# Delta and differential attention in one stage of 49 slots, with a level's pairs formed and copied ahead of the first half turn

## What the reference computes

```python
h = rms_norm_2(x, pre_mix_w[l]); u = h @ w_in[l]
y_conv  = conv_module(...)
y_diff  = diff_attention(dq, dk, dv, lambdas..., l)     # 6 heads, 12 maps of width 32
y_delta = gated_deltanet(gqkv, gz, b_f, b_b, a_f, a_b, ...)   # 6 heads, two directions
x = x + rms_norm_2(concat(y_conv, y_diff, y_delta) @ w_out[l], ...)
x = x + rms_norm_2(square(relu(rms_norm_2(x) @ w_ff1)) @ w_ff2, ...)
```

```python
p = softmax(s - slopes[:, None, None] * dist); a = p[:, :, 0] - lam * p[:, :, 1]
o = einsum("bhqk,bkhe->bqhe", a, vf)
```

## Time and profile before

| what | value |
|---|---|
| median of 3 runs | 4210.27 us (4207.33 to 4212.7) |
| span of the profiled execution | 4209.9 us |
| PE busy | 3901.8 us (93%) |
| PEld busy | 3126.2 us (74%) |
| DVE busy | 2270.4 us (54%) |
| ACT busy | 1414.5 us (34%) |
| POOL busy | 237.8 us (6%) |
| mean granted TensorE clock | 0.943 |

### The profile page before, as it was taken

How to read it: one execution, slowest core, us unless ns; L and a number is a source line. 1 busy time by engine, 2 the same in 40 slices (tenths; PEclk the granted TensorE clock), 3 DMA queues, 4 the chain that set the end, 5 groups by cost and what they waited for, 6 DMA issues and landing times. The chain is left out here.

```text
span 4209.9 us, 49789 instructions
## 1 busy us (share of the span) xinstructions
PE 3901.8 (93%) x20649; PEld 3126.2 (74%) x20649; DVE 2270.4 (54%) x3424; ACT 1414.5 (34%) x2074; POOL 237.8 (6%) x212
## 2 busy tenths in 40 slices
PE   7998799999999999899999989889998989898998
PEld 4884667888888777578877778557786768666876
DVE  5625755554564333362267666753475856664375
ACT  2115633111443121252254222432364322343264
POOL 0000210000000000000000032000000023000000
PEclk9998889999999999999999999789999989799998
DMA  5500013343112111123232100022232200012231
GB/s 203 171 31 10 6 41 100 128 134 117 57 56 83 58 58 58 40 81 100 82 100 84 53 4 1 6 71 90 90 100 68 69 7 1 6 61 70 90 100 60
DMA packets 254721, 288.90 MB, mean 69 GB/s; under 512 B 6757, under 2 KB 226940, under 8 KB 254518
## 3 DMA queue, kind: packets, MB, share of 16 engines
q1 hardware_dynamic: 252437, 281.84, 20.8%
q10 hardware_dynamic: 2080, 4.19, 0.3%
HBM read 283.92 MB, written 2.10 MB: 68 GB/s over the span
## 5 line engine op out<-in xcount | busy, mean ns | idle before, releaser
L458 PE MATMUL banks<-h_halves,w_halves 128*128 128x512 f32 x3824 | 1437.4, 376 | 83.1 <-DVE h_halves L257 42.2
L459 PE MATMUL banks<-h_halves,w_halves 128*128 128x512 f32 x3824 | 1429.7, 374 | 0.0
L460 PE MATMUL banks<-h_halves,w_halves 128*128 128x512 f32 x3824 | 1422.9, 372 | 0.0
L458 PEld LDWEIGHTS banks<-h_halves,w_halves 128*128 128x128 f32 x3824 | 735.1, 192 | 234.7 <-issue 84.9
L460 PEld LDWEIGHTS banks<-h_halves,w_halves 128*128 128x128 f32 x3824 | 732.4, 192 | 127.8
L459 PEld LDWEIGHTS banks<-h_halves,w_halves 128*128 128x128 f32 x3824 | 734.6, 192 | 121.1 <-issue 0.5
L257 DVE TENSOR_TENSOR w_halves<-work,w_halves 128x2048 fp32r<-128x2048 f32 (+1 forms) x215 | 488.2, 2271 | 468.7 <-ACT w_halves L252 468.4
L252 ACT ACTIVATE w_halves<-work 128x2048 fp32r<-128x2048 f32 (+1 forms) x215 | 407.2, 1894 | 535.7 <-PE banks L460 401.9
L252 ACT ACTIVATE h_halves<-kept 128x512 fp32r<-128x512 f32 (+1 forms) x520 | 332.5, 666 | 313.4 <-PE banks L460 234.8
L257 DVE TENSOR_TENSOR h_halves<-kept,h_halves 128x512 fp32r<-128x512 f32 (+1 forms) x520 | 361.2, 736 | 138.6 <-ACT h_halves L252 137.9
L950 DVE SCALAR_TENSOR_TENSOR kept<-kept 128x512 f32<-128x512 f32 x280 | 188.2, 744 | 7.7 <-DMA kept<-in_mod_w 7.7
(11 more groups left out here) (367 smaller groups left out, 4548.4 us busy)
## 6 DMA issues: line engine op xcount, KB each, us to landing
work<-in_w_ff SPq DMA_DIRECT2D x64, 1024.0 KB, 5.4
work<-in_ffn_w_in SPq DMA_DIRECT2D x44, 1024.0 KB, 5.1
kept<-in_mod_w SPq DMA_DIRECT2D x40, 1024.0 KB, 5.2
work<-in_odd_w_in SPq DMA_DIRECT2D x24, 1024.0 KB, 5.1
work<-in_w_in SPq DMA_DIRECT2D x24, 1024.0 KB, 5.2
work<-in_ffn_w_out SPq DMA_DIRECT2D x16, 1024.0 KB, 5.2
work<-in_even_w_in SPq DMA_DIRECT2D x13, 1024.0 KB, 5.3
work<-in_odd_w_out SPq DMA_DIRECT2D x8, 1024.0 KB, 5.2
```

The lines of the kernel that those rows point to most:

```text
L458: nc.tensor.matmul(o, low[:, k - a, fc], rh[:, tc], start=(k == 0), stop=False)
L459: nc.tensor.matmul(o, high[:, k - a, fc], rl[:, tc], start=False, stop=False)
L460: mm = nc.tensor.matmul(o, high[:, k - a, fc], rh[:, tc], start=False, stop=(k == K - 1))
```

## The change

`diff_stage` is gone and `delta_stage` becomes `mixer_stage`, which carries the 24 attention steps in the 49 slots: a step starts every second slot. With `step_at(t, lag)`, slot t does the scores of step (t + 2) / 2 at its end, the maximum and the exponentials one slot later, the scaling and the subtraction two later, the turns three later, the weighing four later. Every step's turn is made in two parts of two transposes through half a bank, each copied by ScalarE.

PSUM banks are dealt anew: pairs and products share one whole bank (they had two halves of two banks), the turned blocks have one bank (before: two), preparation and outputs one each, the small state products one in all (before: two, alternating), attention three. So a level is no longer cut in halves, except for the turn, whose second half waits until ScalarE has emptied the bank.

The level's mask is applied on GpSimd ahead of time to the Gram matrix (`masked_level`), and VectorE's masking of the pairs is replaced by a copy of the pairs on ScalarE (`pairs_copy`). The first level's pairs are a transpose. In a slot TensorE issues pairs, half turn 0, half turn 1; ScalarE copies pairs, half 0, half 1. The scaling of the second map and the copying out of results go from VectorE to ScalarE. The dummy matmuls are gone. A set has 50 semaphores. The split operands and the buffers of attention get new places in SBUF.

```diff
+PAIR0 = U0 + 26 * SEQ
+    level_bank, x_bank, prep_bank, out_bank = (core.ps[:, b, :] for b in range(4))
+    score_bank = lambda m: core.ps[:, 5 + m, :]
+    turn_bank = core.ps[:, 7, 0:2 * P]
...
+            def pairs(h, lv):
+
+                m = level_of(h, lv)
+                pe.wait_ge(level_masked, m + 1)
+                if m:
+                    pe.wait_ge(u_done, m)
+                for c in range(4):
+                    o, s = level_bank[:, cc(c)], pl.level[m % 3][:, cc(c)]
+                    if lv:
+                        mm = nc.tensor.matmul(packed(o, lv), s, chunk_blocks(h, lv, c), start=True, stop=True)
+                    else:
+                        mm = nc.tensor.transpose(o, s, core.ident())
                 mm.then_inc(pt_done, 1)
...
             def turn(h, lv, e):
 
+                pe.wait_ge(u_done, level_of(h, lv))
+                if turn_of(h, lv, e):
+                    pe.wait_ge(x_done, turn_of(h, lv, e))
...
+            prepare(0, 0)
+            pe.wait_ge(v_copied, 1)
+            pe.wait_ge(dist_made, 1)
+            scores(0)
+            for step in range(1, 4):
                 prepare(0, step)
-                for _ in range((1, 1, 2, 0)[step]):
-                    nc.tensor.matmul(core.ps[:, 7, :], core.sb(ONES0, P), core.x(0)[:, LAT], start=True, stop=True)
             for h in range(H + 1):
                 for lv in range(LV):
+                    t = level_of(h, lv)
                     if h < H:
-                        for e in range(2):
-                            pairs(h, lv, e)
+                        pairs(h, lv)
                     if h < H and lv:
-                        for e in range(2):
-                            turn(h, lv, e)
+                        turn(h, lv, 0)
+                    if h < H and lv:
+                        turn(h, lv, 1)
                     before(h, lv)
+                    attend(t, 0)
                     if h < H and lv:
-                        for e in range(2):
-                            products(h, lv, e)
+                        products(h, lv)
                     behind(h, lv)
+                    attend(t, 1)
...
+            for t in range(slots):
+                h, lv = divmod(t, LV)
+                if step_at(t, 4) is not None:
+                    copy(step_at(t, 4), 1)
+                if h < H and lv:
+                    pairs_copy(h, lv)
+                    kept(h, lv, 0)
+                    kept(h, lv, 1)
+                if step_at(t, 2) is not None:
+                    rescale(step_at(t, 2))
+                if step_at(t, 3) is not None:
+                    copy(step_at(t, 3), 0)
+                if step_at(t, 4) is not None:
+                    out(step_at(t, 4))
+                if step_at(t, 1) is not None:
+                    s = step_at(t, 1)
+                    exps(s)
+                    if s in split_at:
+                        split(split_at[s])
...
+            def masked_level(h, lv):
+
+                m = level_of(h, lv)
+                if lv == 0:
+                    pool.wait_ge(s_ready, h + 1)
+                if m >= 3:
+                    pool.wait_ge(pt_done, m - 2)
+                nc.gpsimd.tensor_tensor(c4(pl.level[m % 3]), c4(pl.s[h % 2]), mat(pl.pairs[:, cc(lv)]),
+                                        ALU.mult).then_inc(level_masked, 1)
...
+            def update(h, lv):
+                u = blocks(h, lv)
...
+                nc.vector.tensor_tensor(u, u, packed(level_bank, lv), ALU.subtract).then_inc(u_done, 1)
...
+                if step_at(t, 1) is not None:
+                    top(step_at(t, 1))
+                if step_at(t, 2) is not None:
+                    invert(step_at(t, 2))
...
+                if h < H:
+                    update(h, lv)
+                if step_at(t, 2) is not None:
+                    subtract(step_at(t, 2))
...
-    delta_stage(core, nc, pl)
-    diff_stage(core, nc, a, l)
+    mixer_stage(core, nc, a, l, pl)
```

More of the change, by code:

```diff
@@ L33 @@
 NEG = -1.0e30
-SET = 49
+SET = 50
 GW = 256
@@ L2773, in __init__ @@
         self.u, self.s = [take(1024) for _ in range(3)], [take(512), take(512)]
+        self.level = [take(512) for _ in range(3)]
         self.x, self.pt, self.bm = take(512), take(512), [take(512), take(512)]
@@ new lines, in turn_step, with weigh @@
+            def turn_step(s, part):
+                if part == 0:
+                    pe.wait_ge(subtracted, s + 1)
+                    if s:
+                        pe.wait_ge(out_done, s)
+                else:
+                    pe.wait_ge(turned_copied, 2 * s + 1)
+                for j in range(2):
+                    mm = nc.tensor.transpose(turn_bank[:, cc(j)], pl.both[s % 2][:, cc(2 * part + j)], core.ident())
+                mm.then_inc(turned, 1)
+            def weigh(s):
+                h, i = steps[s]
+                pe.wait_ge(turned_copied, 2 * s + 2)
+                for j in range(4):
+                    mm = nc.tensor.matmul(weigh_bank(half(h)), pl.vt_diff[:, j * DIFF_W + h * HD:j * DIFF_W + (h + 1) * HD],
+                                          pl.at[s % 2][:, cc(j)], start=(j == 0), stop=(j == 3))
+                mm.then_inc(weighted, 1)
@@ new lines, in attend @@
+            def attend(t, place):
+                if place == 0:
+                    for s, work in ((step_at(t, 3), lambda s: turn_step(s, 0)), (step_at(t, 4), weigh)):
+                        if s is not None:
+                            work(s)
+                else:
+                    for s, work in ((step_at(t, 0), scores), (step_at(t, 3), lambda s: turn_step(s, 1))):
+                        if s is not None:
+                            work(s)
+            for b in range(3):
+                for q in range(4):
+                    mm = nc.tensor.transpose(core.ps[:, 5 + b, cc(q)], u2(core, 10 + b)[:, cc(q)], core.ident())
@@ L3104, in _, with out @@
+            def out(s):
+                h, i = steps[s]
+                act.wait_ge(weighted, s + 1)
+                nc.scalar.activation(u2(core, 4 + h // 2)[half(h), cc(i)], weigh_bank(half(h)), ACT.Copy).then_inc(out_done, 1)
+            split(0)
             for step in range(3):
                 prepare(0, step)
[L3106 to L3113 removed]
+            act.wait_ge(lam_s, 1)
```

514 lines of the change are left out of this document (221 added, 293 removed).

## The result

The changed kernel takes 4235.16 us (median of 4; 4229.82 to 4236.18) against 4210.26 us, a ratio of 1.0054 with a 95% interval of 1.004 to 1.0068: slower, by 23 us by the ratio and 25 by the medians. 4225 had been forecast, 15 us above the kernel before.

A forecast was written before the change was run, and what follows sets the result against it. Both stages bound by TensorE's own queue; 26 + 37 + 184 + 43 + 1 + 25 + 3 = 319 us a layer against 312.4, 14 us more in two layers: about 4225 us; range 4182 to 4264.

The forecast's parts named there:

- start to the second level's pairs: Merged stage's start, until the second level's pairs: 8.65 + 2.8 + 11.9 + 1.3 + 1.5 = 26 us, bounds 23 and 29.
- rest of the first head: First head from its second level on, working without a predecessor: 37 us a layer.
- heads 2 to 5: The four middle heads (heads 1 to 4 in the prediction) at 46.0 us each: 184 us a layer.
- last head, end, clock, split: Last head without preparation 43 us, closing chain 25, slow clock after the start 3, third tile's split 1.
- The turn wait: Second half turn waits until ScalarE empties the one bank: 0.66 us in six levels, 4.0 us a head.
- A head: One head of the merged stage: TensorE work 40.4, turn waits 4.0 and slack 1.6, in all 46.0 us.
- 1.6 us of slack: Per head, 0.8 us for short slots and 0.8 for ScalarE's queue delaying the pairs' copy; bounds 0 and 5.
- Mostly beside it: At the start, lambdas, first maximum and its exponentials precede the first update but mostly overlap other work: 1.5 us.
- The idle time is filled: Rival on in-order queues other than the turn wait: spill-over and short slots cost nothing, head 44.4 us, 4186; chance 0.28.
- The sign: Pairs' copy starting within 0.1 us of the pairs' end in nearly all slots was to decide for filled idle time.
- Queues slip more: Rival: ScalarE, or VectorE held back by GpSimd's masks, delays 36 slots by 0.5 us each, 4261; chance 0.14.
- The clock falls: Rival: waits in slots put a tenth of the merged stage at 0.50 clock, 15 us a layer, 4255; chance 0.06.

The follow-up runs named there:

- e1: The changed kernel with the first half turn ahead of the pairs on TensorE and its kept blocks copied ahead of the pairs on ScalarE: 4176.66 us, ratio 0.9929.
- e4: The changed kernel with the merging undone: new delta order kept, attention in its old stage behind it: 4315.28 us, ratio 1.0259.
- e10: e9 with VectorE's start reordered (lambdas first, first maximum ahead of the query Gram products) and ScalarE's exponential of the lambdas ahead of the preparation: 4154.08 us, ratio 0.9870.
- e9: e1 with the distance table and lambda vectors loaded in the stage before, and the dummy matmuls put back: 4165.86 us, ratio 0.9896.
- e6: e1 with dummy matmuls of 512 columns put back at the start: 4169.19 us, ratio 0.9908.
- e3: The changed kernel with each level's mask product done twice on GpSimd, the first time into an unread tile: 4233.11 us, ratio 1.0058.
- e8: e4 with the first half turn ahead of the pairs and its kept blocks ahead of the pairs' copy: 4266.12 us, ratio 1.0134.
- e7: e1 with early loads, five dummies and another order at the start: 4164.17 us, ratio 0.9896.

## Why the prediction was right

Its sum was per layer, so it can be set against the starts of the levels' pairs in the trace after (layer 0 / layer 1):

| term | forecast | measured |
|---|---|---|
| start to the second level's pairs | 26 | 30.5 / 30.2 |
| rest of the first head | 37 | 38.7 / 38.3 |
| heads 2 to 5 | 184 | 185.2 / 184.0 |
| last head, end, clock, split | 72 | 68.6 / 70.3 |
| sum | 319 | 323.0 / 322.8 |

The forecast of the time was 10 us short, and of the change of 23 to 25 us it had 15. In part the terms cancel: start, first head and middle were some 6.5 us a layer too small, end and clock 2.6 too large.

*The turn wait.* 0.66 us in 72 levels, 47.5 us; the trace has 46.7, and e1 takes it away with its consequences. The new order of delta costs 109 us (e4) and the merge brings 86, which leaves a loss; with the 53 us of the order of turns back, the same merge is a gain.

*A head.* 46.0 forecast, 46.1 measured. Of the two heads from 2551.68 to 2643.93 (92.25 us) TensorE was idle for 11.4, of which 7.4 are turn waits and 1.0 the third tile's split: without the 11.4 a head is 40.4 us, the forecast's sum of pieces. The pieces of the earlier trace rows kept their lengths in the new order, so adding them worked. Of the forecast's 1.6 us of slack 1.5 are there, but made up otherwise. It had 0.8 for ScalarE's queue spilling over into the pairs' copy. That does not happen: in 34 of 36 levels of each layer the copy starts 0.03 to 0.04 us after the pairs' end, and the other two (0.3 and 1.04 us) stand behind the splits of the second and third tile. In its place are waits for the update, 1.1 us a head where 0.8 was forecast, and 0.4 for ScalarE elsewhere. That the sum of the two came out is luck.

*The start* is the term that was too small, by 4.3 us a layer. Up to the first level's pairs it was right: 8.65 + 2.8 + 1.3 and 8.7 of the 11.9 are 21.4 us, measured 21.75. The first scores started 0.77 us later than in the old stage (GpSimd's cast of the table began 0.36 us later and took 1.35 us in place of 0.95). From the first to the second level's pairs it was 3.25 us before; with the forecast's 1.5 for lambdas, maximum and exponentials that makes 4.75, and it took 8.72. "Mostly beside it" was wrong: the first update stands behind all of them in VectorE's queue and starts 6.6 us after the pairs. What I had not seen as well is that the second step's scores, 2.5 us at the lower clock, stand in TensorE's queue ahead of the second level's pairs and wait for the first exponentials: the update ends at 2464.38 and the pairs start at 2465.46, so this adds 1.1 us. e10 shows VectorE's part: there the second level's pairs come 6.0 us earlier in each layer than in e9.

*The last head, the end and the clock* together were too large by 2 to 3 us: the attention steps keep TensorE at work, so the last 24 us ran at a clock of 0.86 in layer 0 and 0.81 in layer 1, where the tail in the earlier trace rows had 0.50. The half clock came at the start instead, 27 us. e6 takes part of it away and gains 9 us in both layers, against 6 for all of it in my sum.

*The rivals.* "The idle time is filled": the prediction said that this case decides once the pairs' copy starts within 0.1 us of the pairs' end in nearly all slots. Just that was measured (above), and a head still takes 46.1 us and not 44.4. The sign was badly chosen: it shows that ScalarE is on time, and what keeps a head above 44.4 is the update in the short slots, 1.1 us a head, and what keeps the layer up is the start.

"Queues slip more": e3 excludes GpSimd's masks as a cost of this size. The ground that the prediction gave for it, 614 against 417 ns for a VectorE update, was misread. Two such updates of the first level in the kernel before, with GpSimd idle from 2469.8 to 2483.7:

```profile
2473.08 1.07 DVE L3235 TENSOR_TENSOR work<-work 128x256 f32<-128x256 f32 x2
```
They take the same time there, so 614 ns is the price of that form and not of GpSimd beside it; only the first pair of each layer, beside a mask product, took longer (1.68 us for the two). What contention does can be seen in the changed kernel, by the least, the median and the longest duration in ns:

```profile
L3251 DVE TENSOR_TENSOR work<-work,banks x84: 681/689/1110, 2463.3 to 3719.2; 128x512 f32<-128x512 f32 x84
L3204 DVE SCALAR_TENSOR_TENSOR kept<-kept x48: 702/747/1437, 2464.2 to 3735.7; 128x512 f32<-128x512 f32 x48
```
The update has one operand in PSUM: 72 of its 84 take 0.69 us, and the twelve of the first level 1.07 to 1.11 each, as the two halves together did before. The subtraction has both operands in SBUF: 38 of 48 take 0.70 to 0.75 us, the other ten 1.24 to 1.44, all beside GpSimd's work, and they are off the path. By the Trainium skill (SBUF — State Buffer, "Who interferes with whom") a VectorE instruction with two SBUF inputs contends with a GpSimd instruction that reads SBUF, and one with a single SBUF input does not; the trace agrees.

"The clock falls": not in the merged middle (1.00), but for one short stretch at 2507.64, behind 1.26 us of idle time, where eight instructions of pairs took 2.04 us in place of 1.16; the head around it takes 47.5 us. In e8, where nothing covers the gaps, the clock is 0.92. The sentence of the Trainium skill on small idles between groups of matmuls, which the prediction names, stands in the page's section "A second HAM failure mode: psum-queue depth-cycling", next to the one named.

What failed is a number of the experiments, not of the prediction: how much the new order costs without attention (27 against 51 us a layer). I had taken the mean slot as 5.6 us from TensorE's pieces; in e4 five slots of the first head that have little else to issue all take 5.4 to 5.5 us, which fits the chain products, update, pairs, turns, copy, and the slots with more work in them still hold the waits.

Left open: what TensorE's order alone would give, what the 56 us of e8 consist of, and where the 2 to 3 us outside the stages come from beyond their scatter.

## What to carry to other kernels

When one buffer must be emptied between two halves of a step, put the independent work between the halves in the issuing engine's queue and let the emptying engine take the first half first; here the order alone was worth 53 us of 4235, beside 86 for the merge of two stages. Where all is bound by one in-order engine, add up its pieces from the trace and then walk one slot by the clock for the waits: both together came within 0.25% of the time and 0.1 us of a head, though the change of the whole was forecast at 15 us and measured at 23 to 25. Before a sign is named that tells two cases apart, ask whether it would look different in the other case. A merged start deserves the same walk as the loop: loads, dummies and VectorE's and ScalarE's orders there were worth 25 us (e1 to e10).

## What was not expected of the hardware

How much GpSimd's two-operand products and VectorE's operations with two SBUF operands hold each other up when they meet: two splits took 3.42 us in e7 against 1.28, GpSimd's three products beside them 1.65 to 1.72 us each in place of 1.26, and a subtraction up to 1.44 us against 0.75. On the mean of all subtractions it is only 871 ns against 751 before. And that the same delta stage alone (e8), with waits of up to 1.6 us for the update ahead of its turns, fell to the lower clock again and again, 0.92 on the mean, while with attention in its slots (the changed kernel's middle) it stayed at 1.00.
